# Cached values of the samples: four small products a page on PE, or scaled on ACT, added on POOL and summed on PE once per sample

## What is computed

```python
v_past = cache_v[page_table].reshape(B, -1, DF_HEADS, DF_DV)      # 8 samples, 8 pages of 128 keys, 4 heads of 128
vals = jnp.concatenate([v_past.astype(v.dtype), v], axis=1)
p = jax.nn.softmax(s, axis=-1)
att = p[:, 0] - lam.astype(jnp.float32) * p[:, 1]
return jnp.einsum('bhqk,bkhd->bqhd', att.astype(v.dtype), v)
```

## Time and profile before

| | |
|---|---|
| median of 3 runs | 2102.05 us (2094.48 to 2104.55) |
| profiled execution | 2102.81 us, span 2100.3 us, mean granted TensorE clock 0.921 |
| PE busy | 1797.9 us, 86% of the span |
| DVE busy | 1442.2 us, 69% |
| POOL busy | 870.4 us, 41% |
| ACT busy | 730.3 us, 35% |
| DMA | 620.99 MB, mean 296 GB/s |

### The profile page before, as it was taken

How to read it: one execution, slowest core, us unless ns; L and a number is a source line. 1 busy time by engine, 2 the same in 40 slices (tenths; PEclk the granted TensorE clock), 3 DMA queues, 4 the chain that set the end, 5 groups by cost and what they waited for, 6 DMA issues and landing times.

```text
span 2100.3 us, 22032 instructions
## 1 busy us (share of the span) xinstructions
PE 1797.9 (86%) x7178; PEld 971.8 (46%) x7178; DVE 1442.2 (69%) x3161; ACT 730.3 (35%) x2012; POOL 870.4 (41%) x769
## 2 busy tenths in 40 slices
PE   7978768898897588899878899978999988899885
PEld 5844337686684433345423444533444633335331
DVE  2768635546555577877787778688878687786665
ACT  0121220000001144554445555444555444443441
POOL 3897522222220143444444444444534344443441
PEclk9989869898998689999999999999999999998998
DMA  7453121121124299999999999999999999999996
GB/s 257 159 191 110 51 76 47 42 76 36 46 61 183 91 402 410 422 407 416 382 411 422 410 385 421 406 420 408 398 376 419 404 406 406 421 418 351 408 418 255
DMA packets 103328, 620.99 MB, mean 296 GB/s; under 512 B 12100, under 2 KB 15556, under 8 KB 36272
## 3 DMA queue, kind: packets, MB, share of 16 engines
q0 software_dynamic: 85792, 580.97, 69.4%
q1 hardware_dynamic: 17424, 38.63, 5.0%
HBM read 613.89 MB, written 5.59 MB: 295 GB/s over the span
## 4 chain that ended last, share of the span: by engine, by line
PE 31%; DMA 17%; DVE 13%; issue 3%; ACT 3%; POOL 1%; SPq 0%; POOLq 0%; ACTq 0%; DVEq 0%
PE ps L1600 23%; DMA p_ring<-in_peer_uv_dram,p_idx 17%; DVE p_ring L1820 5%; PE ps L1554 4%; PE ps L1528 2%; PE ps L1498 1%; ACT p_dg L1709 1%; ACT L1703 1%; POOL p_ring L1438 1%; DVE p_x L1743 1%; ACT p_wgt L1705 1%; DVE p_work L1796 1%; DVE p_ia L1797 0%; DVE p_x L1747 0%; DVE p_work L1794 0%
## 5 line engine op out<-in xcount | busy, mean ns | idle before, releaser
L1600 PE MATMUL ps<-p_ring,p_dg 128*128 128x512 f32 x2048 | 977.6, 631 | 164.3 <-ACT p_dg L1709 157.3
L1438 POOL DMA_INDIRECT p_ring<-in_peer_uv_dram,p_idx x512 | 585.9, 1144 | 839.1 <-PE ps L1600 713.0
L1820 DVE CUSTOM_DVE_ANT_0 p_ring<-p_ring,p_x 128x1024 f32<-128x1024 f32 x512 | 616.7, 1225 | 290.0 <-DMA p_ring<-in_peer_uv_dram,p_idx 285.6
L1600 PEld LDWEIGHTS ps<-p_ring,p_dg 128*128 128x128 f32 x2048 | 399.4, 201 | 704.9 <-issue 436.6
L1703 ACT ACTIVATE p_gel<-p_dot 128x1 f32<-128x1 f32 x512 | 103.5, 202 | 591.5 <-DVE p_dot L1820 590.2
L1709 ACT ACTIVATE p_dg<-table_long,p_wgt 128x128 f32<-128x128 f32 x512 | 206.1, 402 | 16.6
L1705 ACT ACTIVATE p_wgt<-p_gel,p_gate 128x1 f32<-128x1 f32 x512 | 151.3, 296 | 16.7
L1024 POOL DMA_INDIRECT vring<-in_cache_v_dram,idx x64 | 61.0, 952 | 147.9 <-PE ps L885 146.2
L275 PE MATMUL ps<-xT,w_ring 128*128 128x268 f32 x448 | 105.5, 400 | 10.6 <-DMA xT<-in_xT_dram 6.4
L300 PE MATMUL ps<-w_ring,xT 128*128 128x512 f32 (+1 forms) x224 | 106.7, 633 | 3.7 <-ACT kv L402 3.7
L275 PEld LDWEIGHTS ps<-xT,w_ring 128*128 128x128 f32 x448 | 87.6, 196 | 28.6 <-issue 6.3
(11 more groups left out here) (362 smaller groups left out, 2091.3 us busy)
## 6 DMA issues: line engine op xcount, KB each, us to landing
w_ring<-in_w_in_dram SPq DMA_DIRECT2D x5, 2048.0 KB, 9.1
p_ring<-in_peer_uv_dram,p_idx POOLq DMA_INDIRECT x512, 10.2
w_out<-in_w_out_dram SPq DMA_DIRECT2D x2, 2048.0 KB, 10.5
wq<-in_pk_wq_dram SPq DMA_DIRECT2D x1, 4096.0 KB, 22.6
xT<-in_xT_dram SPq DMA_DIRECT2D x4, 536.0 KB, 6.2
kv<-in_w_in_dram SPq DMA_DIRECT2D x1, 2048.0 KB, 12.5
w_out<-q_rows POOLq DMA_DIRECT2D x8, 256.0 KB, 3.8
p_x<-in_x_tok_dram SPq DMA_DIRECT2D x4, 512.0 KB
```

What stands on the lines that cost most here:

```text
L1438: pool.indirect_dma_start(out=dst, out_offset=None, in_=io[table], in_offset=bass.IndirectOffsetOnAxis(ap=at, axis=0)).then_inc(s_to, 16)
L1600: mm = pe.matmul(acc[:, a, :], dg[:, j % DG, :], Vr[:, j % R, a * 512:(a + 1) * 512], start=(at == 0), stop=(at == SLOTS - 1), skip_group_ ...
L1820: dve.tensor_tensor_reduce(Ur[:, r, :], Ur[:, r, :], x, 1.0, 0.0, ALU.mult, ALU.add, dot[:, j % RC:j % RC + 1]).then_inc(s_dot, 1)
```

## The change

Each page is now weighed before PE sees it. ACT multiplies each head's 128 columns of a page by that head's weight per key (`own_pages`, four copies with a pointer scale, in place). POOL adds the scaled pages of a sample up (`add_pages`): the first page of a sample lands in one of two buffers `total`, the other seven land in `vring` and are added to it, and behind each add POOL fetches the next page. PE then adds over the keys once per sample (`own_sum`): one product of 512 columns whose stationary operand is a window of `picked`, a column of ones between zeros. `zatt`, `spread_weights` and `own_page` go. The first page of a sample waits for PE's sum of the sample two back.

ACT's pages stand in its queue at five points of a tile: 4 at its start, ahead of the square root and mixed copy; 2 behind each of the four copies of `token_major`; 1 behind AV's copy; 3 behind W's. POOL's adds of the tile's first 4 pages stand ahead of XT's first value, the other 12 behind it. The sum of a tile's first sample stands in its second chunk, that of its second sample in level 0 of the next tile, and the last one behind the last gate. The first five pages are fetched at the start of the phase. SP's load of the output weights also waits for the last sum, as `total` lies in `m.w_out`.

```diff
-        zatt = free[:, 2 * RWW:2 * RWW + NPG * NH * ZW].rearrange("p (g h z) -> p g h z", g=NPG, h=NH)
+        total = free[:, 0:2 * RWW].rearrange("p (a n) -> p a n", a=2)
+        picked = free[:, 2 * RWW:2 * RWW + ZW]
...
-        s_zr, s_vuse, s_so, s_soc = sem("zr"), sem("vuse"), sem("so"), sem("soc")
-        s_kv = m.s_page[0:VR]
+        s_att, s_scaled, s_added, s_summed = sem("att"), sem("scaled"), sem("added"), sem("summed")
+        s_so, s_soc = sem("so"), sem("soc")
+        s_kv, s_kv0 = m.s_page[0:VR], m.s_page[VR:VR + 2]
+
+        def place(p):
+            b, g = divmod(p, NPG)
+            if g == 0:
+                return total[:, b % 2, :], s_kv0[b % 2], KEYS_DONE + 16 * (b // 2 + 1)
+            n = (NPG - 1) * b + g - 1
+            return vring[:, n % VR, :], s_kv[n % VR], KEYS_DONE + 16 * (n // VR + 1)
...
+            sp.wait_ge(s_summed, NB)
...
                 for l in range(len(levels)):
-                    own_page(ti)
+                    if l == 0 and ti >= 2:
+                        own_sum(2 * ti - 3)
...
                     if ti:
-                        own_page(ti)
+                        if ch == 1:
+                            own_sum(2 * ti - 2)
                         state_products(ti - 1, ch)
...
+            def own_sum(b):
+                if b == 0:
+                    pe.wait_ge(s_att, 1)
                     for h in range(NH):
                         mm = pe.matmul(ps[0:NB, 1, h * DV:(h + 1) * DV], attD[:, :, h], m.vtok[0:NB, NT, h * DV:(h + 1) * DV],
                                        start=(h == 0), stop=False, skip_group_check=True)
                     mm.then_inc(s_so, 1)
+                pe.wait_ge(s_added, (NPG - 1) * (b + 1))
+                pe.matmul(ps[0:NB, 1, :], picked[:, NB - 1 - b:2 * NB - 1 - b], total[:, b % 2, :], start=False, stop=(b == NB - 1),
+                          skip_group_check=True).then_inc(s_summed, 1)
...
             gate(slice(TP, TA), NB, 5, DH)
+            own_sum(NB - 1)
             pe.wait_ge(s_soc, 1)
...
+            def token_major(ti, q):
+                act.wait_ge(s_tr, 4 * ti + q + 1)
+                act.activation(tok[0:n, ti % 2, q, :], ps[0:n, 0, :], ACT.Copy).then_inc(s_trc, 1)
+            def own_pages(ti, first, end):
+                for p in range(16 * (ti - 1) + first, 16 * (ti - 1) + end):
+                    b, g = divmod(p, NPG)
+                    page, landed, count = place(p)
+                    act.wait_ge(landed, count)
+                    for h in range(NH):
+                        hs = slice(h * DV, (h + 1) * DV)
+                        ins = act.activation(page[:, hs], page[:, hs], ACT.Copy, scale=attB[:, g, b, h:h + 1])
+                    ins.then_inc(s_scaled, 1)
+            for q in range(4):
+                token_major(0, q)
...
                 n = tiles[ti][1]
+                if ti == 1:
+                    act.wait_ge(s_att, 1)
+                if ti:
+                    own_pages(ti, 0, 4)
                 if ti >= 2:
                     root(ti - 1)
                     mixed(ti - 1)
-                if ti + 1 < NTL:
-                    token_major(ti + 1)
+                for q in range(4):
+                    if ti + 1 < NTL:
+                        token_major(ti + 1, q)
+                    if ti:
+                        own_pages(ti, 4 + 2 * q, 6 + 2 * q)
                 act.wait_ge(s_AV, ti + 1)
                 act.activation(AV[0:n, :], ps[0:n, 0, :], ACT.Copy).then_inc(s_AVc, 1)
+                if ti:
+                    own_pages(ti, 12, 13)
                 act.wait_ge(s_UW, ti + 1)
                 if ti:
                     act.activation(WT[:, :, :], ps[:, 2, :].rearrange("p (i t) -> p i t", i=HP), ACT.Copy).then_inc(s_UWc, 1)
+                    own_pages(ti, 13, 16)
                 else:
                     act.activation(stmp[:, 0, 0:1], c("ident")[:, 0:1], ACT.Copy).then_inc(s_UWc, 1)
-            act.wait_ge(s_vuse, NPAGES)
+            act.wait_ge(s_summed, NB)
             act.activation(os, ps[0:NB, 1, :], ACT.Copy).then_inc(s_soc, 1)
             act.wait_ge(s_first_dve, 1)
             for a in range(2 * NH):
...
+            fetched = iter(range(NPAGES))
+            def fetch():
+                for p in fetched:
+                    b, g = divmod(p, NPG)
+                    page, landed, count = place(p)
+                    if g == 0 and b >= 2:
+                        pool.wait_ge(s_summed, b - 1)
+                    n = (NPG - 1) * b + g - 1
+                    if g and n >= VR:
+                        pool.wait_ge(s_added, n - VR + 1)
+                    pool.indirect_dma_start(out=page, out_offset=None, in_=io["cache_v"],
+                                            in_offset=bass.IndirectOffsetOnAxis(ap=m.idx[:, p:p + 1], axis=0)).then_inc(landed, 16)
+                    if g:
+                        return
+            def add_pages(ti, first, end):
+                for p in range(16 * (ti - 1) + first, 16 * (ti - 1) + end):
+                    b, g = divmod(p, NPG)
+                    if g == 0:
+                        continue
+                    n = (NPG - 1) * b + g - 1
+                    pool.wait_ge(s_scaled, p + 1)
+                    if g >= 2:
+                        pool.wait_ge(s_added, n)
+                    pool.tensor_tensor(total[:, b % 2, :], total[:, b % 2, :], place(p)[0], ALU.add).then_inc(s_added, 1)
+                    fetch()
+            for i in range(VR):
+                fetch()
             for ti in range(NTL):
                 n = tiles[ti][1]
                 if ti:
+                    add_pages(ti, 0, 4)
...
                     ins.then_inc(s_vd, 1)
+                    add_pages(ti, 4, 16)
...
-            dve.memset(zatt[:, :, :, :], 0.0)
+            link(dve.memset(picked, 0.0))
+            link(dve.memset(picked[:, NB - 1:NB], 1.0))
...
-                link(dve.tensor_reduce(attB.rearrange("p g b h -> p (g b h)"), ps[:, 2, :].rearrange("p (x y) -> p x y", y=2), AX.X, ALU.add))
-                spread_weights(0)
+                link(dve.tensor_reduce(attB.rearrange("p g b h -> p (g b h)"), ps[:, 2, :].rearrange("p (x y) -> p x y", y=2), AX.X, ALU.add), s_att)
-                    if ti + 1 < NTL:
-                        spread_weights(4 * ti)
```

More of the change, by code:

```diff
@@ L866, in sample_weights @@
                           start=True, stop=True).then_inc(s_sT, 1)
-            pages = iter(range(NPAGES))
-            def own_page(ti):
-                if not ti:
-                    return
-                p = next(pages)
-                b, g = divmod(p, NPG)
-                if g % 4 == 0:
-                    pe.wait_ge(s_zr, p // 4 + 1)
-                if p == 0:
+            def own_sum(b):
+                if b == 0:
+                    pe.wait_ge(s_att, 1)
                     for h in range(NH):
@@ L882, in own_page @@
                     mm.then_inc(s_so, 1)
-                pe.wait_ge(s_kv[p % VR], KEYS_DONE + 16 * (p // VR + 1))
-                for h in range(NH):
-                    mm = pe.matmul(ps[0:NB, 1, h * DV:(h + 1) * DV], zatt[:, g, h, NB - 1 - b:2 * NB - 1 - b],
-                                   vring[:, p % VR, h * DV:(h + 1) * DV], start=False, stop=(p == NPAGES - 1), skip_group_check=True)
-                mm.then_inc(s_vuse, 1)
+                pe.wait_ge(s_added, (NPG - 1) * (b + 1))
+                pe.matmul(ps[0:NB, 1, :], picked[:, NB - 1 - b:2 * NB - 1 - b], total[:, b % 2, :], start=False, stop=(b == NB - 1),
+                          skip_group_check=True).then_inc(s_summed, 1)
             for q in range(4):
@@ L964, in mixed @@
                                ACT.Copy).then_inc(s_mtc, 1)
-            def token_major(ti):
+            def token_major(ti, q):
                 n = tiles[ti][1]
-                for q in range(4):
-                    act.wait_ge(s_tr, 4 * ti + q + 1)
-                    act.activation(tok[0:n, ti % 2, q, :], ps[0:n, 0, :], ACT.Copy).then_inc(s_trc, 1)
-            token_major(0)
+                act.wait_ge(s_tr, 4 * ti + q + 1)
[11 more added lines that the diff above has]
+                token_major(0, q)
             act.wait_ge(s_smx, 1)
@@ L1019, in _ @@
         def _(pool):
-            def fetch(p):
-                if p >= VR:
-                    pool.wait_ge(s_vuse, p - VR + 1)
-                pool.indirect_dma_start(out=vring[:, p % VR, :], out_offset=None, in_=io["cache_v"],
-                                        in_offset=bass.IndirectOffsetOnAxis(ap=m.idx[:, p:p + 1], axis=0)
-                                        ).then_inc(s_kv[p % VR], 16)
+            fetched = iter(range(NPAGES))
[25 more added lines that the diff above has]
+                fetch()
             for ti in range(NTL):
@@ L1030, in _ @@
                 if ti:
-                    for p in range(16 * ti - 16, 16 * ti - 12):
-                        fetch(p)
+                    add_pages(ti, 0, 4)
```

(3 more changed lines are left out.)

11 lines of the change are left out of this document (removed).

## The result

The changed kernel takes 2080.09 us (median of 8 runs, 2072.38 to 2085.54) where the kernel before, timed beside it, takes 2101.15 (8 runs, 2094.48 to 2109.79): a ratio of 0.9892, 95% interval 0.9864 to 0.992; by the medians 21 us less. Timed again later it had 0.9917 (0.9888 to 0.9947). The two profiled executions, which the prediction's sum is made for, differ by 17.5 us of span (2100.3 and 2082.8). The forecast was 2088, 14.7 off; its direction held, but several of its terms were wrong in size, and the loss by PE's granted clock was not in the sum at all.

A forecast was written before the change was run, and what follows sets the result against it. PE was taken to lead the second phase, busy 73.1 of a tile's 82.6 us. Terms 22 + 1.6 - 5 - 2 - 1.9 = 14.7 us off 2102.81 gave 2088, range 2070 to 2107.

The forecast's parts named there:

- Levels: Levels 1 to 4 of each tile: without pages each takes 6.78 us for 8.13, gaining 1.35, with a new 0.6 gap.
- The second page of level 0: Level 0 of a tile: the first page was hidden already, removing the second gains 0.97 us.
- Tile 1: Tile 1: POOL's adds ahead of XT make T products 4.8 us later, leaving a gain of 6.4 - 4.8 = 1.6.
- Refill: Tiles 2 to 4: POOL's next-sample fetches and pages take 17.5 us, leaving 10 us before XT is due; costs nothing.
- Rival 3: Tiles 2 to 4: POOL's refill delays XT and ACT's square root, making the kernel slower, 2115 us; chance 0.08.
- Collisions: Chunks and tile starts: POOL's adds delay DVE operations with both operands in SBUF; 5 us lost, bounds 0 and 13.
- Opening: Start of second phase: five first pages fetched beside the samples' state load cost 2 us, bounds 0 and 3.4.
- Tail: Before L917: last sum 0.97, ACT's copy 0.59 and handovers 0.3 cost 1.9 us.
- Rival 4: Levels: PE's new 0.6 us gaps bring its granted clock down, giving 2130 us and more; chance 0.02.
- beside DVE's U: Chunks and outputs: the second and fourth pages stand beside DVE's U, so removing them gains nothing.
- Rival 1: Second phase: little gain left after collisions, opening and level start pages; 2104 us, down to 2094; chance 0.24.
- rival 2: Second phase: PE sets the pace throughout, all 54 us go less 13.7 of other terms; 2062 us; chance 0.07.

The follow-up runs named there:

- e4: Changed kernel plus four products with zeros ahead of the X and XT products in all five levels of tiles 1 to 4; tiles and tail 330.9 us for 304.1.
- e1: Changed kernel with POOL making tile 1's XT starts before adding pages 1 to 3; tile 1 71.17 us for 74.52, tiles and tail 300.8 for 304.1.
- e5: Changed kernel plus four products with zeros at the start of levels 1 to 4 in tiles 1 to 4; tiles and tail 323.2 us for 304.1.
- e6: Changed kernel plus four products with zeros ahead of both chunks' waits for U and ahead of L850; tiles and tail 304.5 us for 304.1.
- e10: Changed kernel with XT first in tile 1, L1172 in level 1, zero products in waits, and sums moved into waits; 2074.79 us, ratio 0.9876 to the kernel before.
- e8: Changed kernel with L1172 moved from the start of tiles 2 to 4 into level 1; tiles and tail 310.1 us for 304.1.
- e9: Changed kernel with L1172 moved into level 1 and zero products ahead of both chunks' U waits and the outputs; tiles and tail 298.4 us for 304.1.
- e3: Changed kernel with POOL adding only 8 of each page's 512 columns, rest of the sum left out; tiles and tail 301.5 us for 304.1.

## Why the prediction was right, and where it was not

By its own steps, for the profiled executions (14.7 forecast, 17.5 measured):

- Levels: 1.35 forecast, 1.51 measured, 2.6 over sixteen levels. The gap and its cause are as forecast; the products into X and XT take 3.57 (425.12 to 428.69), not the 3.77 read behind a page. The 0.2 more that e4 shows for a page in this place belongs to the page and was counted with the products. The second page of level 0 is worth the same 1.17 for 0.97, 0.6 in tiles 2 to 4.
- Tile 1: T was forecast to come 4.8 later. Its second half starts 16.28 behind the weights' row (338.01 and 321.73) where it started 13.22 behind (332.89 and 319.67), so 3.1 later; the 3.64 of e1 are counted from e1's own, earlier start. Then level 0 loses 1.7 to the half clock, which makes 4.8. The number is right by luck. ACT scales a page in 1.2 us, not 1.6: four copies of 0.39 overlap when they follow each other.

```profile
322.43 1.28 ACT L979 ACTIVATE w_out<-w_out 128x128 f32<-128x128 f32 x4 [8.12 <-DVE w_out L1231]
323.62 3.60 ACT L979 ACTIVATE vring<-vring,w_out 128x128 f32<-128x128 f32 x12
```

- Refill: 10 us to spare were forecast for XT; POOL waited 11.65 for DVE's mask ahead of tile 4's XT. Nothing, as said. Rival 3 did not come in any run.
- Collisions: 5 forecast, 2.9 measured (L1172 1.58 and 0.09, L1165 0.4 in each of three tiles; L1162 was 0.27 longer in tile 4, and its chunk was not). The finish steps, where the prediction put some of them, met no add in the changed kernel. The average hides what is there: each depends on the phase of POOL's adds to a few tenths of a microsecond.
- Opening: 2 forecast, 1.9. Tail: 1.9 forecast, 1.6; L917 waits for ACT's copy:

```profile
625.81 1.25 PE L917 MATMUL ps<-kv,qT 64*128 64x144 f32 x16 [0.68 <-ACT AV L1014]
```

- Not in the sum: the half clock, 3.1 us in the outputs of tiles 1 and 3, beside the 1.7 in tile 1's level 0. Rival 4 had the mechanism, in the levels and at 28 us or more. It came in one level, and in the chunks and outputs, where the pages had stood "beside DVE's U" and were costed at nothing. That is the step which failed: a page which hides in a wait was counted as free to remove. Its removal costs no time at that place, but it leaves PE waiting, and PE can then be slower behind it.

Against the forecast, levels and level 0's pages give 3.2 more, collisions 2.1, opening and tail 0.4, and the half clock in the outputs takes 3.1: 2.6 more in all, where 2.8 more was measured. So the total was near because errors of both signs met. Rival 1 (nothing left) and rival 2 (PE paces all) fall by the level rows and e5.

## What to carry to other kernels

A piece of work that hides in a wait of TensorE is not free to take out: look at what the granted clock does behind the wait once it is empty, and if it falls, try products with zeros in the wait (in e6 tiles 2 and 4, which had kept their clock, got longer by no more than their collisions). Work moved to POOL meets those operations of DVE that keep their operands in SBUF; what it costs depends on their phase, so ask which operations of DVE lead at that moment and move them where DVE waits, before counting an average. Equal tiles that differ in time are worth a look of their own, since two losses can hide each other from tile to tile.

## What the runs showed of the hardware

- An operation of DVE with both operands in SBUF that began 0.54 or more into POOL's issue of an indirect DMA waited also through the add behind it: 2.27, 2.05 and 2.23 us instead of 0.69 and 0.68. One that began 0.33 into the issue did not wait, and the issue got longer instead (1.12 for 0.96); both are in the changed kernel, in chunk 2 of tile 1 L1165 inside an add and L1166 inside a fetch:

```profile
384.59 1.10 DVE L1165 TENSOR_TENSOR S<-S,qks 128x512 f32<-128x512 f32 x1
385.72 0.69 DVE L1166 TENSOR_TENSOR qks<-S,w_out 128x512 f32<-128x512 f32 x1
...
383.85 1.27 POOL L1066 TENSOR_TENSOR w_out<-w_out,vring 128x512 f32<-128x512 f32 x1
385.39 1.12 POOL L1052 DMA_INDIRECT vring<-in_cache_v_dram,idx  x1 [0.27 <-POOL w_out L1066]
```

- A small operation (L1199 of e10, 128x8) took 0.96 instead of 0.17 and ended 0.03 behind POOL's add. The Trainium skill (SBUF — State Buffer, "SBUF: two separate sides") has the port pair held for a whole instruction by whichever begins first; that DVE, begun at 472.57, did not get it before the add of 473.01 is not what that sentence alone gives. Counting from the fetch of 472.03 does not settle it either, since L1166 began inside a fetch and was not held. POOL's fetch took 1.33 instead of 0.96 beside L1200 of e10.
- The half clock comes in the chunks and outputs in stretches of 3 to 20 us behind waits of PE of 0.9 to 1.4 us. The longest, in e5 and e8, begin ahead of the chunks, behind a wait of 0.85 for XT where the page after the levels had stood. It comes in tiles 1 and 3 of the changed kernel in each of its three profiles, in tile 4 in one of them, and in other tiles after a change as small as one operation of DVE. With the waits ahead of U and L850 filled by products with zeros (e6, e9), or by such products and the sums (e10), it stayed at full in twelve tiles of twelve; why tiles with the same empty waits differ stays open.
- The third phase, unaltered in all kernels, took 1401 us (e3) to 1424 us (e9) from its first load to the end of the span. That is the size of the whole effect, and what makes it was not found.
